# Layer boundaries with both norms from three sums per output tile, in a two-layer block followed by a second block

## The chip, the cores and the metric

One core of a Trainium2 chip runs the whole program in one launch. The metric is device time in microseconds of that core, from the start of the program to its end. The engines that matter here are TensorE (PE, matrix products), VectorE (DVE), ScalarE (ACT), GpSimd (POOL) and the DMA queues, above all SyncE's (SP), which streams the weights.

## What is computed

256 tokens of x and 256 tokens of ctx, 1024 features, two layers of a three-branch block (attention, a long convolution, a gated MLP), and then one layer of a second block on x alone. Everything is float32. What matters here lies where a layer ends and the next begins:

```python
for l in range(DEPTH):
    h  = rms_norm(x,  norm_pre[l]) * (1.0 + sc[:, None]) + sh[:, None]
    hc = rms_norm(xc, norm_pre[l]) * (1.0 + scc) + shc
    z  = h @ w_in[l]
    ...
    out   = merge_branches(z, (y_a, y_b, y_c), w_branch[l], w_out[l])   # ends with "out @ wo"
    x_new = x + gt[:, None] * rms_norm(out, norm_post[l])
    if not last:
        xc = xc + gtc * rms_norm(outc, norm_post[l])
    x = x_new
...
proj = rms_norm_2(x, g_mix[i]) @ w_in[i]      # second block, on x
```

So at each boundary there are two norms over the 1024 features of every token: one of the branch's output, and one of the new x, which is the old x plus the gated, normalized output.

## The kernel before

**Layout.** Activations lie with features on the 128 partitions: x is `self.x[:, k, :]`, k = 0 to 7 (KT = 8) blocks of 128 features, with 512 columns (ALL): 256 tokens of x (TOK), then 256 of ctx. Layer 0 works on 512 columns, layer 1's output and block 2 on 256. Weights come as tiles of 128 x 1024 in one fixed stream. `plan()` writes their order; a Tile has a number t, a kind ("wout", "q", "k", "v", "zc", "head", "cmp" ...) and a number of use, whose remainder by 4 is its PSUM bank among gemm_bank0 to 3. misc_bank0 to 3 (`self.M`) serve for the rest.

**Products in three parts.** Each float32 product is done as three in a rounded format (`three`, L417 to L419): both operands are split into hi and lo. For a weight tile SyncE loads `raw` (4 buffers, a load waits until the split four tiles before is done), ScalarE writes `whi` (`act_hi`, L1190; it waits until the tile four before is used up), VectorE writes `wlo` (`dve_lo`, L1711). ScalarE is three tiles ahead of TensorE, VectorE two.

**Programs.** Each engine has its own instruction list, written out by hand as one Python walk (`pe_...`, `act_...`, `dve_...`, `pool...`). `mark` increments a semaphore with an instruction, `at` gives the value that another engine waits for. An engine works in the order of its list, so a wait holds up all that follows on that engine. `pe_tiles(n)`, `act_tiles(n)` and `dve_tiles(n)` do the next n tiles' work on each engine; with `split=False` without the weight split ahead. A bank is free for a new tile when the copy out of it is done (`pe_bank`: it waits for "evac" of the use four before).

**End of a layer.** `pe_block1` runs eight wout tiles. ScalarE squares each (`act_sq`) and writes the gated output to `branch_out` (in the `halves` buffer); GpSimd adds the squares of tiles 0 to 6 (`pool_sums`, L2534), and TensorE sums over partitions with the constant `mean_all` (`pe_pooled`, L626 and L628). Beside the wout tiles of layer 0 there are tiles of kind "ada" (four products each pair, in four partition groups of one bank, L506) and the parts of layer 1's convolution filter: hidden layers, four taps (`pe_taps`, L663), squares, tap norm (`pe_tap_norm`, L677), spectrum (`pe_spec`, L694, and `dve_kern`).

**Boundary 0 to 1** (`pe_cross`, `act_cross`, `dve_cross`), first the x half (s = 0), then the ctx half (s = 1). VectorE takes reciprocals of the 256-column roots (L2224), scales the output and adds it to x for eight feature blocks (`dve_cross_new`, L2231 and L2232), ScalarE squares the new x (L1496), TensorE sums (L744), root, reciprocal, and then for each k VectorE forms the scaled input (L2239), ScalarE adds the shift and rounds (`act_cross_h`, L1505), VectorE writes the lo half (L2245). The four query tiles take the x half alone and go in the order QUAD, which starts tile after tile as the blocks k arrive; the four key tiles take both halves, in the order CROSS_KEYS of (tile, half). In `act_cross` each of four rounds squares some blocks and then does `act_tiles(1)`: one weight copy and one query bank copied out. After the keys come the four value tiles with tokens on the partitions, each of which writes all four banks, the angles and ropes on VectorE (`dve_trig`, `dve_rope`, L1975 to L1978), and the scores (L812), which wait for the last rope.

**Boundary 1 to block 2.** The same steps for 256 columns (L2314 and L2315, `act_sq`, `pe_sum` at L620, `dve_hn` at L2214 and L2218). `pe_block2` begins with waits for three constants (head_spread, ck_w2, cv_w2) that GpSimd loads (L2560 to L2562) behind its wait for the last "x_new", since their place held other data until then; then tiles zc 0, zc 1, head 0, 1, 2, with a sum for each head (`pe_head`, L974), and the compress tiles, for which ScalarE and VectorE first make up their other operand (`act_pair`, `dve_compress`).

Of the kernel before, what the change touches and what calls it, by code (L numbers as in the profile page):

```python
# [14 lines left out]
P = 128  # L15
# [18 lines left out]
CROSS_SUMS = (18, 20, 22, 24, 25, 27, 29, 31)  # L34
CROSS_SQ = ((0, 1, 2, 3, 4), (5,), (6, 7), ())
CROSS_KEYS = ((0, 0), (1, 0), (2, 0), (0, 1), (1, 1), (3, 0), (2, 1), (3, 1))
# [58 lines left out]
def plan():  # L95
# [33 lines left out]
    for l in range(DEPTH):  # L129
# [40 lines left out]
        if l == 0:  # L170
            extra["spec", 1] = uses
            uses += 1
# [45 lines left out]
POOLED = (("out", 0), ("out", 1), "g_ffn")  # L218


class Kernel:
# [82 lines left out]
    def memory(self):  # L304
# [24 lines left out]
        self.modA = sb("modA", [P, KT, 2])  # L329
        self.subg = [sb(f"sub_gain{l}", [P, 1]) for l in range(DEPTH)]  # L330
# [81 lines left out]
    def branch_out(self, k, s):  # L412
        return self.halves_f[:, k, s * ALL:s * ALL + TOK]

# [70 lines left out]
    def pe_tile(self, T):  # L485
# [25 lines left out]
        elif kind in ("k", "q", "hy", "gu", "gate", "esel", "zc", "head", "wout", "wout2", "pgate"):  # L511
            begun = {"k": ("h", T.l), "wout": ("merged", T.l), "zc": ("hn", "g_mix"), "wout2": ("merged", 2), "pgate": ("hn", "g_ple")}.get(kind)
# [130 lines left out]

    def hid(self, l):
        return self.tmp[0:64, 3, 0:TOK] if l else self.y[0:64, 0, 0:TOK]
# [9 lines left out]
    def pe_taps(self, l):  # L655
# [3 lines left out]
        for part in range(2):  # L659
            for t in range(2):  # L660
                if l == 0 and part and t:
                    pe.wait_ge(*self.at("root", "x0", 1))
                pe.matmul(self.tap_bank(l, 2 * part + t)[:, :], hid[:, t::2], self.hy_w3[:, part * BR:(part + 1) * BR], start=True, stop=True).then_inc(*self.mark("pe_filter", "taps_mm", l, 2 * part + t))  # L663

    def tap_bank(self, l, i):
        return self.M[i if l else (i + 1) % 4]
# [13 lines left out]
    def spec_bank(self, l, i):  # L680
        if l == 0:
            return self.M[i]
        return self.M[1 + i] if i < 3 else self.G[self.extra["spec", 1] % 4]

    def pe_spec(self, l):
        pe, sd = self.pe, self.tap_rows(l)[2]
        pe.wait_ge(*self.at("tap_root", l))
        pe.wait_ge(*self.at("tap_sd", l))
        pe.wait_ge(*self.landed("dft"))
        for part in range(2):  # L690
            for par in range(2):
                if l and part and par:
                    self.pe_bank(self.extra["spec", 1])
# [47 lines left out]
    def pe_cross_sum(self, s, k):  # L741

        self.pe.wait_ge(*self.at("sq", ("res", 0, s), k))
        self.pe.matmul(self.M[0][:, self.half(s)], self.c["mean_all"], self.tmp[:, k % 2, self.half(s)], start=(k == 0), stop=(k == KT - 1)).then_inc(*self.mark("pe_sum", "summed", ("res", 0, s), k))  # L744

    def pe_cross_queries(self, tiles):

        n = 0
        for step, (i, k) in enumerate(QUAD):
# [10 lines left out]
            if step in CROSS_SUMS:  # L760
                self.pe_cross_sum(1, CROSS_SUMS.index(step))

# [17 lines left out]
    def pe_cross(self):  # L780

        queries, keys = self.tiles[self.pe_next:self.pe_next + 4], self.tiles[self.pe_next + 4:self.pe_next + 8]
        for k in range(KT):
            self.pe_cross_sum(0, k)
        self.pe_cross_queries(queries)
        for i, side in CROSS_KEYS:
            self.pe_cross_keys(keys[i], side, (i, side) == (0, 1))
        self.pe_next += 8

    def pe_first(self):  # L790
# [3 lines left out]
        self.pe_tiles(2)  # L794
        self.pe_tap_norm(0)
# [134 lines left out]
    def pe_block1(self, l):  # L930
# [15 lines left out]
        for o in range(KT):  # L946
# [11 lines left out]
        if l == 0:  # L958
            self.pe.wait_ge(*self.at("taps", 1))
        self.pe_sum(("out", l), KT - 1, n)  # L960
        if l == 0:
            self.pe_tap_norm(1)
            self.pe_spec(1)
            self.pe_cross()
            return
        self.pe.wait_ge(*self.at("rstd", ("out", l)))
        for k in range(KT):
            self.pe_sum(("res", l), k, n)
# [103 lines left out]
    def pe_block2(self):  # L1072
# [5 lines left out]
        pe.wait_ge(*self.at("rstd", ("res", 1)))  # L1078
        self.pe_tiles(2)
        self.pe_heads(3)  # L1080
# [1720 lines left out]
```

## Time and profile before

| | |
|---|---|
| median of 3 timed runs | 1439.62 us (1439.2 to 1440.12) |
| profiled execution, its own time | 1443.96 us |
| its span | 1442.6 us, 20879 instructions |
| TensorE busy | 1381.1 us (96%), weight loads beside it 1166.8 us |
| VectorE, ScalarE, GpSimd busy | 936.2 (65%), 688.9 (48%), 41.8 us (3%) |
| granted TensorE clock, mean | 0.981 of 2.4 GHz |

Times in the profile are microseconds from the span's start. A line such as L1711 is that of the instruction in the kernel; where a helper issues all of one kind, one line stands for many. In a timeline each row gives the start, the duration, the engine, the line and operation, output <- inputs by the program's names, shapes and a count of merged instructions, and in brackets how long the engine was idle before it and what ended that. Matrix products overlap: one of 512 columns in the rounded format lasts 0.39 us, and the next starts 0.23 us after it; with 256 columns 0.28 and 0.12. A float32 product stands as two instructions. Layer 0 ends at 627 us and layer 1 at 970 us.

### The profile page before, as it was taken

How to read it: one execution, taken by the hardware profiler on the slowest of the kernel's cores; microseconds unless marked ns; L12 is line 12 of the kernel's file. 1: busy time of each engine (PE TensorE's matmuls, PEld its weight loads, DVE VectorE, ACT ScalarE, POOL GpSimd, SP SyncE). 2: the span in 40 equal slices, each digit the busy share in tenths (PEclk: the TensorE clock that was granted, in tenths of full speed). 3: DMA queues.
4: the chain of work that ended last, by engine and by line, in shares of the span. 5: the costliest groups of instructions: out<-in, count | busy, mean ns of one | idle time of the engine just before them, and what ended most of it. 6: DMA issues, size and time to landing. Idle time of an engine off the chain costs nothing.

```text
span 1442.6 us, 20879 instructions
## 1 busy us (share of the span) xinstructions
PE 1381.1 (96%) x8318; PEld 1166.8 (81%) x8318; DVE 936.2 (65%) x1687; ACT 688.9 (48%) x1190; POOL 41.8 (3%) x50
## 2 busy tenths in 40 slices
PE   5999999999999999989999999998999999999998
PEld 2577668778888888669789899997889999888888
DVE  4574664876423344388875777658867777888556
ACT  5433545234322232454356454465656746666444
POOL 0000000000000000100000000010000002000001
PEclk8999999999999999999999999998999999999999
DMA  9332343144332232622233355553633245655552
GB/s 364 137 102 73 144 148 103 44 171 158 102 102 88 90 100 81 215 77 89 78 126 133 124 191 194 186 176 109 212 136 116 92 145 176 199 186 193 197 175 74
DMA packets 57793, 202.21 MB, mean 140 GB/s; under 512 B 6272, under 2 KB 9536, under 8 KB 57696
## 3 DMA queue, kind: packets, MB, share of 16 engines
q1 hardware_dynamic: 55568, 194.01, 39.9%
q0 software_dynamic: 1760, 6.12, 1.3%
q8 instruction: 66, 1.08, 0.3%
q10 hardware_dynamic: 368, 0.74, 0.2%
q14 instruction: 31, 0.25, 0.1%
HBM read 199.80 MB, written 1.05 MB: 139 GB/s over the span
## 4 chain that ended last, share of the span: by engine, by line
PE 83%; DVE 10%; ACT 3%; DMA 2%; issue 1%; ACTq 0%; SPq 0%; DVEq 0%
PE gemm_bank L417 16%; PE gemm_bank L419 15%; PE gemm_bank L418 15%; PE misc_bank L417 4%; PE misc_bank L418 4%; PE misc_bank L419 4%; PE misc_bank L428 3%; PE gemm_bank L428 3%; DVE wlo L1711 2%; PE gemm_bank L573 1%; PE misc_bank L573 1%; PE misc_bank L429 1%; PE gemm_bank L429 1%; PE gemm_bank L506 1%; PE misc_bank L853 1%; PE misc_bank L812 1%
## 5 line engine op out<-in xcount | busy, mean ns | idle before, releaser
L1711 DVE TENSOR_TENSOR wlo<-raw,whi 128x1024 fp32r<-128x1024 f32 x316 | 382.9, 1223 | 76.6 <-ACT whi L1190 73.2
L1190 ACT ACTIVATE whi<-raw 128x1024 fp32r<-128x1024 f32 x316 | 332.8, 1055 | 163.1 <-PE gemm_bank L419 95.8
L417 PE MATMUL gemm_bank<-halves,wlo 128*128 128x256 f32 (+1 forms) x1152 | 376.5, 327 | 18.7 <-DVE halves L2175 5.2
L418 PE MATMUL gemm_bank<-halves,whi 128*128 128x256 f32 (+1 forms) x1152 | 361.4, 314 | 0.0
L419 PE MATMUL gemm_bank<-halves,whi 128*128 128x256 f32 (+1 forms) x1152 | 361.3, 314 | 0.0
L417 PEld LDWEIGHTS gemm_bank<-halves,wlo 128*128 128x128 f32 x1152 | 223.6, 194 | 42.6 <-issue 17.8
L419 PEld LDWEIGHTS gemm_bank<-halves,whi 128*128 128x128 f32 x1152 | 224.0, 194 | 12.0
L418 PEld LDWEIGHTS gemm_bank<-halves,whi 128*128 128x128 f32 x1152 | 224.4, 195 | 11.3 <-issue 0.7
L417 PE MATMUL gemm_bank<-arena_r,wlo 128*128 128x512 f32 (+1 forms) x320 | 108.3, 338 | 1.9 <-DVE wlo L1711 1.9
L419 PE MATMUL gemm_bank<-arena_r,whi 128*128 128x512 f32 (+1 forms) x320 | 107.6, 336 | 0.0
L418 PE MATMUL gemm_bank<-arena_r,whi 128*128 128x512 f32 (+1 forms) x320 | 107.5, 336 | 0.0
L417 PE MATMUL misc_bank<-halves,wlo 128*128 128x512 f32 (+1 forms) x288 | 101.9, 354 | 0.0
L418 PE MATMUL misc_bank<-halves,whi 128*128 128x512 f32 (+1 forms) x288 | 101.9, 354 | 0.0
L419 PE MATMUL misc_bank<-halves,whi 128*128 128x512 f32 (+1 forms) x288 | 101.9, 354 | 0.0
L1746 DVE SCALAR_TENSOR_TENSOR tmp<-tmp,gemm_bank 128x512 f32<-128x512 f32 (+1 forms) x28 | 16.1, 574 | 97.4 <-ACT tmp L1259 97.4
L1259 ACT ACTIVATE tmp<-misc_bank 128x512 f32<-128x512 f32 (+1 forms) x36 | 19.0, 527 | 121.3 <-PE misc_bank L419 121.3
L417 PEld LDWEIGHTS gemm_bank<-arena_r,wlo 128*128 128x128 f32 x320 | 60.7, 190 | 11.2 <-DVE wlo L1711 3.5
L419 PEld LDWEIGHTS gemm_bank<-arena_r,whi 128*128 128x128 f32 x320 | 60.7, 190 | 6.3
L418 PEld LDWEIGHTS gemm_bank<-arena_r,whi 128*128 128x128 f32 x320 | 60.8, 190 | 6.1
L428 PE MATMUL gemm_bank<-halves,whi 128*128 128x512 f32 x176 | 62.2, 395 | 0.0
L428 PE MATMUL misc_bank<-halves,whi 128*128 128x512 f32 x176 | 62.1, 394 | 0.0
L417 PEld LDWEIGHTS misc_bank<-halves,wlo 128*128 128x128 f32 x288 | 54.5, 189 | 7.5
(419 smaller groups left out, 2271.8 us busy)
## 6 DMA issues: line engine op xcount, KB each, us to landing
raw<-in_stream SPq DMA_DIRECT2D x348, 512.0 KB, 3.3
arena<-in_stream SPq DMA_DIRECT2D x16, 512.0 KB, 11.6
x<-in_x SPq DMA_DIRECT2D x1, 1024.0 KB, 6.8
x<-in_ctx SPq DMA_DIRECT2D x1, 1024.0 KB, 10.2
y<-in_hy_decay POOLq DMA_DIRECT2D x2, 512.0 KB, 4.1
arena<-in_gm_ws POOLq DMA_DIRECT2D x2, 512.0 KB, 5.8
const_b<-in_const_b POOLq DMA_DIRECT2D x1, 635.0 KB, 5.8
y<-in_hy_w POOLq DMA_DIRECT2D x2, 256.0 KB, 3.5
```

Source lines behind the costliest of these rows:

```text
L417: mm(out, w_lo, r_hi, start=first, stop=False)
L418: mm(out, w_hi, r_lo, start=False, stop=False)
L419: return mm(out, w_hi, r_hi, start=False, stop=last)
L428: self.pe.matmul(bank[:, :], hi[:, c], self.hi_lo(k, s), start=(k == 0), stop=False)
L429: m = self.pe.matmul(bank[:, 0:TOK], lo[:, c], self.hi(k, s), start=False, stop=(k == KT - 1))
L506: m = pe.matmul(bank[c:c + 32, :], self.cond_w[:, 2 * q + kk, :], raw[:, kk * BR:(kk + 1) * BR], start=(q < 2), stop=(q >= 2), tile_positi ...
L573: pe.matmul(self.out_banks[o][:, :], hi[:, c], self.ah_al[:, j, :], start=(j == 0), stop=False)
L812: mm = pe.matmul(self.M[m][:, 0:nkeys], self.Q[r, h, q], self.K[r, h, k_off:k_off + nkeys], start=True, stop=True)
L1190: act.activation(self.whi[:, t % SPLIT, :], self.raw_tile(t), ACT.Copy).then_inc(*self.mark("tile_hi", "tile_hi", t))
L1259: act.activation(self.tmp[:, e % 2, 0:n], self.M[e][:, 0:n], ACT.Tanh, scale=0.5).then_inc(*self.mark("act_sel", "sel_tanh", T.use))
L1711: dve.tensor_tensor(self.wlo[:, t % SPLIT, :], self.raw_tile(t), self.whi[:, t % SPLIT, :].bitcast(F32), ALU.subtract).then_inc(*self.mark ...
L1746: self.own(dve.scalar_tensor_tensor(th, th, 1.0, b[:, 0:n], ALU.add, ALU.mult))
```

## The change

Three products per wout tile instead of one square. For the gated output b (after the gate, `branch_out`), the raw output o and the old x, TensorE sums over features o*o, x*b and b*b. They go into the partition groups 0 to 31, 32 to 63 and 64 to 95 of misc_bank0 (`pe_norm_sum`). ScalarE squares o, VectorE forms x*b and b*b one tile later (`dve_branch`). With r = 1/sqrt(mean o*o + eps) the energy of the new x is E(x) + 2 r (x.b) + r^2 (b.b), so the second norm is known as soon as the first is. The three rows are copied to SBUF, transposed so that each token is a partition, and both factors are worked out as columns (`act_norm`, `dve_norm_factors`). Each is spread over all partitions again by a product with the identity (`pe_norm_spread`). E(x) of the input comes from its root once, at the start (`pe_input_energy`, `dve_input_energy`). GpSimd's sums at the two boundaries go, and so do the squares of the new x and their sums.

VectorE then goes block by block: scale b, form the next input, add to x, write the lo half (`dve_cross_rows`, `dve_last_rows`). At the last boundary the first four tiles run in the order QUAD (`pe_last_quad`). The taps are split over two wout tiles, the spectrum over the place before the queries and the place after the keys. The core of the diff:

```diff
-CROSS_KEYS = ((0, 0), (1, 0), (2, 0), (0, 1), (1, 1), (3, 0), (2, 1), (3, 1))
+CROSS_KEYS = ((0, 0), (1, 0), (2, 0), (3, 0), (0, 1), (1, 1), (2, 1), (3, 1))
-POOLED = (("out", 0), ("out", 1), "g_ffn")
+POOLED = ("g_ffn",)
...
+    def pe_norm_sum(self, l, j, n):
+        pe = self.pe
+        for q, src in enumerate(self.norm_rows(j, n)):
+            pe.wait_ge(*self.at(("sq", "xb", "bb")[q], ("out", l), j))
+            m = pe.matmul(self.by_half(self.M[0][32 * q:32 * q + 32, 0:n], n), self.c["mean_all"][:, 0:32], src, start=(j == 0), stop=(j == KT - 1), tile_position=(0, 32 * q))
+        m.then_inc(*self.mark("pe_sum", "summed", ("out", l), j))
+    def pe_norm_turn(self, l, n):
+        self.pe.wait_ge(*self.at("norm_rows", l))
+        for i in range(n // P):
+            m = self.pe.transpose(self.M[0][:, 96 * i:96 * i + 96], self.tmp[0:96, 2, i * P:(i + 1) * P], self.ident[0:96, 0:96])
+    def pe_norm_spread(self, l, s, i):
+        pe.wait_ge(*self.at("norm_r", l, i))
+        if s:
+            pe.wait_ge(*self.at("h", l + 1, 0, KT - 1))
+        for e in range(2):
+            r = self.norm_r[:, 4 * i + 2 * s + e:4 * i + 2 * s + e + 1]
+            m = pe.matmul(self.spread_bank(i)[:, e * P:(e + 1) * P], r.broadcast_to([P, P]), self.ident, start=True, stop=True)
...
     def pe_cross_queries(self, tiles):
-            if step in CROSS_SUMS:
-                self.pe_cross_sum(1, CROSS_SUMS.index(step))
+            if step == 2 * KT + 7:
+                for r in range(2):
+                    self.pe_norm_spread(0, 1, r)
     def pe_cross(self):
-        for k in range(KT):
-            self.pe_cross_sum(0, k)
+        self.pe_norm_turn(0, ALL)
+        self.pe_spec(1, 0, 1)
+        for r in range(2):
+            self.pe_norm_spread(0, 0, r)
         self.pe_cross_queries(queries)
         for i, side in CROSS_KEYS:
             self.pe_cross_keys(keys[i], side, (i, side) == (0, 1))
+        self.pe_spec(1, 1, 2)
...
     def pe_block1(self, l):
             if o:
-                self.pe_sum(("out", l), o - 1, n)
+                self.pe_norm_sum(l, o - 1, n)
             if l == 0 and o == 4:
-                self.pe_taps(1)
+                self.pe_taps(1, range(3))
+            if l == 0 and o == 5:
+                self.pe_taps(1, range(3, 4))
...
     def pe_block2(self):
         pe.wait_ge(*self.landed("head_spread"))
         pe.wait_ge(*self.landed("ck_w2"))
         pe.wait_ge(*self.landed("cv_w2"))
-        pe.wait_ge(*self.at("rstd", ("res", 1)))
-        self.pe_tiles(2)
-        self.pe_heads(3)
+        self.pe_last_quad()
+        self.pe_tiles(1)
+        for n in range(2):
+            self.pe_head(n)
...
+    def act_norm(self, l, n):
+        act.wait_ge(*self.at("summed", ("out", l), KT - 1))
+        act.activation(self.tmp[0:96, 2, 0:n], self.M[0][0:96, 0:n], ACT.Copy).then_inc(*self.mark("act_root", "norm_rows", l))
+        act.wait_ge(*self.at("norm_cols", l))
+        act.activation(self.norm_r[:, 0:n // P], self.norm_cols(0, n), ACT.Sqrt, bias=self.c["eps"]).then_inc(*self.mark("act_root", "root_out", l))
+        act.wait_ge(*self.at("energy", l))
+        act.activation(self.norm_r[:, 4:4 + n // P], self.energy[:, 0:n // P], ACT.Sqrt, bias=self.c["zero"]).then_inc(*self.mark("act_root", "root_new", l))
     def act_cross(self):
+        self.act_norm(0, ALL)
         act.wait_ge(*self.at("mod", 1))
-        self.act_cross_h(0)
+        self.act_cross_h(0, 0, 1)
+        self.act_kern(1, 0)
+        self.act_cross_h(0, 1, KT)
         for i in range(4):
-            for k in CROSS_SQ[i]:
-                self.act_cross_sq(1, k)
-            self.act_tiles(1)
-        act.wait_ge(*self.at("summed", ("res", 0, 1), KT - 1))
-        self.act_cross_root(("res", 0), 1)
-        self.act_cross_h(1)
+            self.act_hi()
+            self.act_cross_h(1, i, i + 1)
+        self.act_tiles(4, split=False)
+        self.act_cross_h(1, 4, KT)
     def act_block1(self, l):
         if l:
             self.act_tiles(1, split=False)
+            self.act_kern(1, 1)
             self.act_tiles(4)
...
+    def dve_branch(self, l, j, n):
+        v, out = self.dve, self.both_halves(j, 0, n)
+        _, xb, bb = self.norm_rows(j, n)
+        for s in range(n // TOK):
+            v.wait_ge(*self.at("branch", l, j, s))
+        if j >= 2:
+            v.wait_ge(*self.at("summed", ("out", l), j - 2))
+        v.tensor_tensor(xb, out, self.by_half(self.x[:, j, 0:n], n), ALU.mult).then_inc(*self.mark("dve_norm", "xb", ("out", l), j))
+        v.tensor_tensor(bb, out, out, ALU.mult).then_inc(*self.mark("dve_norm", "bb", ("out", l), j))
+    def dve_cross_rows(self, s):
+        v = self.dve
+        v.wait_ge(*self.at("spread_r", 0, s, 0))
+        for k in range(KT + 2):
+            if k < KT:
+                self.dve_scaled(0, s, k)
+            if k == 1:
+                v.wait_ge(*self.at("spread_r", 0, s, 1))
+            if 1 <= k <= KT:
+                self.dve_cross_sum(s, k - 1)
+            if k < KT:
+                self.dve_new(0, s, k)
+            if k >= 2:
+                self.dve_cross_lo(s, k - 2)
+            if s == 0 and k == 4 or s and k < 4:
+                self.dve_lo()
+            if s == 0 and k == 8:
+                self.dve_tap_rs(1)
     def dve_block1(self, l):
         if l:
             self.dve_tiles(6, split=False)
-            self.dve_tiles(2)
+            self.dve_tiles(1)
+            self.dve_kern(1, 1, 2)
+            self.dve_tiles(1)
...
     def gpsimd_program(self):
-            self.pool_sums(("out", l), TOK if l else ALL)
-        pool.wait_ge(*self.at("x_new", DEPTH - 1, KT - 1))
+        pool.wait_ge(*self.at("x_new", DEPTH - 1, 0, KT - 1))
         pool.dma_start(self.head_spread, ins["head_spread"]).then_inc(*self.landing("head_spread"))
```

`dve_last_rows` has the same loop as `dve_cross_rows` for the 256 columns of the last boundary, with one `dve_lo` at k = 5. `pe_last_quad` is the loop of `pe_cross_queries` over the tiles zc 0, zc 1, head 0 and head 1. `act_block2` begins with the rounding of the eight blocks, one weight copy and the copies of the two zc banks. `dve_norm_factors` is a chain of operations on columns: reciprocal, product, product with addition, product, then one addition per group of 128 tokens, and behind ScalarE's second root another reciprocal.

## Rows read from the trace of the kernel before

**Rows 1.** The page: chain by engine; the two costliest groups of other engines.

```profile
PE 83%; DVE 10%; ACT 3%; DMA 2%; issue 1%; ACTq 0%; SPq 0%; DVEq 0%
...
L1711 DVE TENSOR_TENSOR wlo<-raw,whi 128x1024 fp32r<-128x1024 f32 x316 | 382.9, 1223 | 76.6 <-ACT whi L1190 73.2
L1190 ACT ACTIVATE whi<-raw 128x1024 fp32r<-128x1024 f32 x316 | 332.8, 1055 | 163.1 <-PE gemm_bank L419 95.8
```

**Rows 2.** Busy time by stretch; behind POOL the granted clock, DMA share, GB/s.

```profile
643.30:650.00 6.70, 6.66 (x32) 6.67 (x33) 6.52 (x15) 3.06 (x6) 0.00 (x0) 0.53 0.26 81
650.00:657.00 7.00, 7.00 (x54) 6.78 (x53) 5.84 (x16) 2.66 (x6) 0.00 (x0) 1.00 0.00 1
```

**Rows 3.** Timeline, TensorE: start us, duration us, engine line op xcount [idle before <-releaser].

```profile
598.61 0.39 PE L419 MATMUL gemm_bank<-arena_r,whi 128*128 128x512 f32 x1
598.92 1.06 PE L506 MATMUL gemm_bank<-raw,cond_w 128*32 128x512 f32 x8
599.92 0.50 PE L417 MATMUL gemm_bank<-arena_r,wlo 128*128 128x512 f32 x1
...
627.17 1.02 PE L626 MATMUL misc_bank<-sq_sum,const_a 128*128 128x512 f32 x2
...
628.98 0.95 PE L677 MATMUL misc_bank<-const_a,arena 128*128 128x1 f32 x8
630.28 2.84 PE L694 MATMUL misc_bank<-y,shared 128*128 128x512 f32 x6 [0.35 <-ACT hy_rs L1341]
...
643.34 0.55 PE L417 MATMUL gemm_bank<-halves,wlo 128*128 128x256 f32 x1 [4.15 <-DVE halves L2245]
```

**Rows 4.** Timeline, VectorE, around the end of layer 0.

```profile
616.54 0.68 DVE L1872 TENSOR_TENSOR arena<-misc_bank,y 128x512 f32<-128x512 f32 x1
...
631.99 0.43 DVE L2232 TENSOR_TENSOR x<-x,halves_f 128x256 f32<-128x256 f32 x1
632.34 0.42 DVE L2231 TENSOR_TENSOR halves_f<-halves_f,tmp 128x256 f32<-128x256 f32 x1
...
643.12 0.48 DVE L2239 SCALAR_TENSOR_TENSOR tmp<-x,modA,tmp 128x256 f32<-128x256 f32 x1
643.51 0.48 DVE L2245 SCALAR_TENSOR_TENSOR halves<-tmp,mod,halves 128x256 fp32r<-128x256 f32 x1
```

**Rows 5.** Timeline, ScalarE, last wout tile of layer 0.

```profile
627.86 1.02 ACT L1270 ACTIVATE halves_f<-gemm_bank,const_a,mod 128x256 f32<-128x256 f32 x2
```

**Rows 6.** Timeline, VectorE and TensorE, from the keys' end to the scores.

```profile
680.22 1.80 DVE L1850 SCALAR_TENSOR_TENSOR tmp<-tmp 128x256 f32<-128x256 f32 x4
683.21 1.23 DVE L1711 TENSOR_TENSOR wlo<-raw,whi 128x1024 fp32r<-128x1024 f32 x1 [1.18 <-ACT whi L1190]
...
684.24 0.40 PE L417 MATMUL gemm_bank<-whi,halves 128*128 128x512 f32 x1
...
709.63 0.70 PE L812 MATMUL misc_bank<-arena 64*128 64x512 f32 x2 [3.44 <-DVE arena L1978]
```

**Rows 7.** Timeline, layer 1 to block 2; one row of the DMA issues.

```profile
970.14 0.59 PE L626 MATMUL misc_bank<-sq_sum,const_a 128*128 128x256 f32 x2
...
979.83 0.42 DVE L2315 TENSOR_TENSOR x<-x,halves_f 128x256 f32<-128x256 f32 x1
...
981.63 0.54 POOL L2562 DMA_DIRECT2D shared<-in_cv_w  x1
...
shared<-in_cv_w POOLq DMA_DIRECT2D x1, 64.0 KB, 3.1
...
985.98 0.55 PE L417 MATMUL gemm_bank<-halves,wlo 128*128 128x256 f32 x1 [3.87 <-DVE halves L2218]
...
994.44 0.39 ACT L1222 ACTIVATE arena<-gemm_bank 128x256 f32<-128x256 f32 x1 [1.53 <-PE gemm_bank L419]
...
1001.10 0.38 ACT L1277 ACTIVATE tmp<-gemm_bank 128x256 f32<-128x256 f32 x1
...
1003.54 0.47 PE L417 MATMUL gemm_bank<-whi,cmp_xl 128*30 128x256 f32 x1
```

More of the change, by code:

```diff
@@ L658, in pe_taps @@
         pe.wait_ge(*self.landed(f"hy_w3{l}"))
[L659 to L663, printed above, removed]
+        for i in some:
+            part, t = divmod(i, 2)
+            if l == 0 and i == 3:
+                pe.wait_ge(*self.at("root", "x0", 1))
+            if l and i == 3:
+                pe.wait_ge(*self.at("tap_out", l, 0))
+            pe.matmul(self.tap_bank(l, i)[:, :], hid[:, t::2], self.hy_w3[:, part * BR:(part + 1) * BR], start=True, stop=True).then_inc(*self.mark("pe_filter", "taps_mm", l, i))
     def tap_bank(self, l, i):
-        return self.M[i if l else (i + 1) % 4]
+        return self.M[1 + i % 3 if l else (i + 1) % 4]
     def tap_rows(self, l):
@@ L794, in pe_first @@
         self.pe_tiles(2)
+        self.pe_input_energy()
         self.pe_tap_norm(0)
@@ L1565, in act_block1 @@
             return
-        self.act_root(("out", l), n)
-        for k in range(KT):
-            act.wait_ge(*self.at("x_new", l, k))
-            self.act_sq(("res", l), k, n, self.x[:, k, 0:n]).then_inc(*self.mark("act_sq", "sq", ("res", l), k))
+        self.act_hi()
+        self.act_norm(1, TOK)
     def act_pair(self, which, z):
@@ L1784, in dve_tile @@
                 self.dve_half("g_ffn", j - 1, 1)
+        elif kind == "wout":
+            if j:
+                self.dve_branch(l, j - 1, n)
         elif kind == "ffg":
@@ L1874, in dve_taps @@
                 self.own(m)
-                v.memset(a[0:1, 2, :], 0.0)
-        m.then_inc(*self.mark("dve_filter", "taps", l))
+                m = v.memset(a[0:1, 2, :], 0.0)
+            if l and i == 0:
+                m.then_inc(*self.mark("dve_filter", "tap_out", l, i))
+        if 3 in some:
+            m.then_inc(*self.mark("dve_filter", "taps", l))
     def dve_tap_add(self, l):
@@ L2225, in dve_cross_rstd, with dve_scaled @@
         self.dve.wait_ge(*self.at("rstd", stage, s))
[L2227 to L2240 removed]
+    def dve_scaled(self, l, s, k):
+        out = self.branch_out(k, s)
+        self.dve.tensor_tensor(out, out, self.spread_bank(0)[:, 0:TOK], ALU.mult).then_inc(*self.mark("dve_x", "out_scaled", l, s, k))
@@ new lines, in dve_new, with dve_cross_sum @@
+    def dve_new(self, l, s, k):
+        x = self.x[:, k, self.half(s)]
+        self.dve.wait_ge(*self.at("out_scaled", l, s, k))
+        self.dve.tensor_tensor(x, x, self.branch_out(k, s), ALU.add).then_inc(*self.mark("dve_x", "x_new", l, s, k))
+    def dve_cross_sum(self, s, k):
+        self.dve.wait_ge(*self.at("x_new", 0, s, k))
+        self.dve.scalar_tensor_tensor(self.tmp[:, (0, 1, 3, 4)[k % 4], self.half(s)], self.x[:, k, self.half(s)], self.modA[:, k, s:s + 1], self.spread_bank(1)[:, 0:TOK], ALU.mult, ALU.mult).then_inc(*self.mark("dve_h", "h_sum", 1, s, k))
@@ L2251, in dve_cross @@
[L2251 to L2264 removed]
+        self.dve_norm_factors(0, ALL)
@@ new lines, in dve_last_rows @@
+    def dve_last_rows(self):
+        v = self.dve
+        self.dve_branch(1, KT - 1, TOK)
+        self.dve_lo()
+        self.dve_norm_factors(1, TOK)
+        v.wait_ge(*self.at("spread_r", 1, 0, 0))
+        for k in range(KT + 2):
+            if k < KT:
+                self.dve_scaled(1, 0, k)
+            if k == 1:
+                v.wait_ge(*self.at("spread_r", 1, 0, 1))
+            if 1 <= k <= KT:
+                self.dve_last_sum(k - 1)
+            if k < KT:
+                self.dve_new(1, 0, k)
+            if k >= 2:
+                self.dve_last_lo(k - 2)
+            if k == 5:
+                self.dve_lo()
+        self.dve_lo()
@@ L2310, in dve_block1 @@
             return
-        self.dve_rstd(("out", l), n)
-        for k in range(KT):
-            out = self.branch_out(k, 0)
-            self.own(v.tensor_tensor(out, out, self.tmp[:, 2, 0:n], ALU.mult))
-            v.tensor_tensor(self.x[:, k, 0:n], self.x[:, k, 0:n], out, ALU.add).then_inc(*self.mark("dve_x", "x_new", l, k))
     def dve_compress(self, which):
```

204 lines of the change are left out of this document (109 added, 95 removed).

## The prediction

> **What bounds the kernel now.** I read the page first. TensorE (PE) holds 83% of the chain that ended last and VectorE (DVE) 10% [rows 1], so a microsecond added to TensorE's program counts in full, and one taken from another engine counts only where TensorE waits for it. The waits of TensorE then show where that is. At the end of layer 0 the last wout tile is through at 627.17, which I call A, and the first product of layer 1 starts at 643.34, A+16.2 [rows 3]. In between come the pooled sum, a reciprocal of 256 columns, eight pairs of "scale, add", eight squares with their sums, and two more reciprocals. After it the granted clock is 0.53 for some six microseconds, that is mostly the lower level of 1.2 GHz, then 1.00 [rows 2]; the engine had waited 4.15 us just before. A stretch of six microseconds at the lower level costs about 2.7 us of the work that it holds. At the end of layer 1 the last wout tile is through at 970.14, which I call B, and the first product of block 2 starts at 985.98, B+15.8 [rows 7]. A third wait hangs on the first: VectorE works from 683.21 without a gap (splits, angles, ropes) up to the last rope, for which the scores wait 3.44 us; they start at 709.63, 25.4 us after the keys ended at 684.24 [rows 6].
>
> **Sums inside wout.** Before, GpSimd added the squares. After, TensorE makes three 512-column products behind each output tile. The nearest row is the pair of ada tiles: four products into four partition groups, eight instructions. The tile before is through at 598.84 (its last product's start and the 0.23 us from one to the next), the next tile's first product starts at 599.92 [rows 3]. The first of the eight lasts as long as one, so the groups run side by side. I take 1.1 us for three; side by side without any cost of changing over it would be 0.85 (the 512-column sum begun at 627.17), one behind the other 2.55. Seven lie ahead of A: +7.7 us. Tile 6's sum also waits. VectorE after tile 5 must do the last tap product, two tap sums, a split (1.22, [rows 1]) and two products of 0.68 [rows 4], 8.6 us in all, against 7.9 us of TensorE work: +0.7. Layer 1 has 256 columns: 7 x 0.6 = +4.2. The sum of the input's energy adds four products like L677's, 0.95 [rows 3]: +1.0, beside nothing. Together +13.6 us (9 to 29).
>
> TensorE's page in the Trainium skill ("TensorE: Matmul & The Clock Gate", Measured speedup vs the span model) gives 2.38 times for three column groups, and its tiling page ("TensorEngine Tiling (Array Packing)", Key Properties) says that a change of mode drains the engine. By the first an estimate is 2.55/2.38 = 1.07 us a group; the second would come on top, but the ada row holds such a change already.
>
> **From A to the first rows of layer 1.** ScalarE (ACT) writes both halves in 1.02 us [rows 5], VectorE multiplies twice (A+2.6), the last sum ends at A+3.6, then copy, four transposes, root, reciprocal (A+5.4). TensorE meanwhile runs two spectrum products (three took 2.55 us, [rows 3]) and spreads the first factor at A+7.0, the second at A+7.6. Nothing of 256 columns is left of roots and reciprocals. VectorE now works in rows: scale 0.35, layer input 0.40, add 0.34, split 0.40 [rows 4], 1.49 us a row, and the first row is whole three rows in: A+10.8 instead of 16.2. That is the gain. But the old program made these rows at 0.79 us each once begun, so the eighth row comes at A+21.0 (with one weight split between), before it was A+22.5. The queries end at A+26.9 (11.5 us of work, starved at first and then partly at the lower clock).
>
> **The keys must wait for the queries' banks.** This is the step that decides. In act_cross the four query banks are now copied out by act_tiles(4) behind four rounds of "act_hi, act_cross_h(1, i)", where before one was copied in each round. The keys take those same banks. Their rows for the second half start when TensorE has spread that half's factors, behind step 23 of the queries: about A+24.0 (22.5 to 25). VectorE scales and adds row 0 and splits key 0's weights: +2.05. Each further round is scale 0.35, layer input 0.48, ScalarE's rounding 0.5, its weight copy 1.05 and VectorE's split 1.22 [rows 1], with the handovers 3.65 us; three of them, then the fourth layer input, rounding and one copy (1.75): the first bank is free at +14.75, A+38.8. TensorE has nothing from A+26.9, 12 us. Then come eight half tiles and again the lower clock (2.7). Half a tile takes 2.88 us: from 643.34 to 684.24 the old program did twelve of them, eight sums of 0.43 (half the columns of the 0.85) and the clock's 2.7 [rows 3, 6]. So the keys end at A+64.5. Before, they ended at A+57.1. **+7.4 us** (3 if no clock is lost and the spread comes early, 9 at the other end).
>
> **Values and ropes.** The second half of the spectrum now follows all keys (1.7 us), and ScalarE's kern copy stands in act_block1 ahead of the first weight copy of the values. So their weights, ready before the keys' end in the old program, are copied from the keys' end+2.5 on and split by +4.8; TensorE waits 3 us. Behind that, VectorE has kern 1.3, a split 1.2, the angles 3.5 (four steps of 1.80 together and five of a third) and then the same gapless 26.4 us up to the scores [rows 6]: 3.6 + 1.2 + 1.3 + 1.2 + 3.5 + 26.4 = keys' end+37.2, where it was +25.4. The value tiles are done by +27, so the scores' wait grows from 3.4 to some 10 us. **+11.8 us** (10 to 13), the 1.7 and the 3 included. What hid them before was that VectorE began them 1.0 us ahead of the keys' end; now it is 10.8 us behind it.
>
> **Block 2.** Here the four first tiles go through pe_last_quad as rows come (first row B+8.6, eighth B+18.7). But pe_block2 still begins with the waits for head_spread, ck_w2 and cv_w2, which GpSimd loads only behind the last x_new. Before, that was 980.25, the last DMA was issued at 981.63 and landed 3.1 us later, 984.7, ahead of the rows; it cost nothing [rows 7]. Now the last x_new stands in round 7 of the row loop: B+16.9, with a landing at B+21.4. TensorE starts at B+21.6, not at B+15.8, with all rows there, and needs 14.2 us for four tiles (11.5 and 2.7 of clock): B+35.8, before B+29.9. ScalarE, too, can copy the first bank only after that tile's end, and from the second bank's copy (994.44) to the end of head 1's square (1001.48) it needed 7.0 us [rows 7]; from B+33.9 with two mask copies of 0.5 that is B+41.4, and TensorE's two head sums wait for it. The compress tiles start at B+41.8, before at 1003.54, B+33.4: **+8.4 us** (5.5 to 10). A later wait of 2 us for loads may shrink: -1.
>
> **Sum.** 13.6 + 7.4 + 11.8 + 8.4 - 1 = 40.2 us. The profiled execution had a span of 1442.6 us and a time of 1443.96; the three timed runs have a median of 1439.62, 0.3% less, which I take as the same shift for both kernels: 1439.6 + 40.2 = 1480.
>
> **Rivals.** (1) Each late wait above is off the path, and the change does what its design wants. Then the keys end at A+53 (the weight splits and the last row at A+44 decide), the second spectrum costs 1.7 on TensorE, the ropes' wait of 3.4 us goes, and block 2 has its four tiles by B+23.5, 6.4 earlier: 13.6 - 4.1 + 1.7 - 3.4 - 6.4 = +1.4, 1441 us, no change; with sums at 0.85 us instead of 1.1 and no fall of the clock at either start (2.7 each) it is faster, 1433. For it speaks the row at A+10.8; against it, that bank, copy and load each stand in one engine's program order. It decides from the point where the first query bank is copied before A+30. Chance 0.07, half of it with a gain that can be measured. (2) One of the three big waits does not come or is given back later (the bank, the ropes, or the loads): 1458 to 1472. Chance 0.15. (3) The three sums run one after the other: 7 x 1.45 in layer 0 and 7 x 0.7 in layer 1, +15 us, 1495. Against it speaks the ada row. Chance 0.06. My forecast, 1472 to 1490, has 0.72.
>
> Range 1456 to 1491; it leaves out most of rival 1 and of rival 3 and holds a little over 8 in 10. A measurement of this kernel can tell about 0.2% (2.9 us) from no change. Faster 0.04, same 0.04, slower 0.92.
>
> **What would show it.** In the profile after: a group of three 32-column products at about 1.1 us behind each wout tile; the first product of layer 1 some 11 us after the last wout tile; a gap of 10 to 13 us ahead of the first key product, ended by ScalarE's copy of a query bank; some 3 us ahead of the first value product, ended by a weight split; some 10 us before the scores, ended by a rope; and a first product of block 2 that starts when cv_w2 has landed, 4.5 us after the last x_new. If the key gap is under 3 us, or the first product of block 2 comes near B+9, I am wrong by the amounts given.

## The result and the profile after

The changed kernel takes 1476.32 us (median of 4 runs, 1474.22 to 1481.52), the kernel before 1439.41 beside it: a ratio of 1.0259 with a 95% interval of 1.0233 to 1.0284, so 2.6% slower. Run again later, the changed kernel gave 1477.5 us and 1.0246 (1.0224 to 1.0268). The profiled execution has a span of 1473.5 us, its own time is 1474.9.

The waits of TensorE in the changed kernel, between 560 and 740 us and between 960 and 1060 us (what waited, for what, us in total, times, longest):

```profile
PE gemm_bank L433 <- ACT arena L1291: 10.8, 1, 10.8
PE misc_bank L862 <- DVE arena L2084: 7.2, 1, 7.2
...
PE gemm_bank L433 <- DVE wlo L1773: 2.9, 1, 2.9
...
PE gemm_bank L433 <- DMA shared<-in_ck_w: 14.7, 1, 14.7
```

The first is the wait for the copy out of a query bank, the second that for the last rope (3.44 before [rows 6]), the third the value weights' split, the last the constants that GpSimd loads. All four are where the prediction put them, at the sizes it gave but for the rope's (some 10 us predicted, 7.2 measured). The instructions at their ends, and the start of layer 1 (timeline, TensorE):

```profile
629.82 0.62 PE L665 MATMUL misc_bank<-tmp,const_a 128*32 128x512 f32 x1
...
636.24 1.44 PE L683 MATMUL misc_bank<-const_a,norm_r 128*128 128x128 f32 x8
640.49 0.36 PE L433 MATMUL gemm_bank<-halves,wlo 128*128 128x256 f32 x1 [2.81 <-DVE halves L2340]
...
651.55 1.05 PE L683 MATMUL misc_bank<-const_a,norm_r 128*128 128x128 f32 x8
...
666.29 0.55 PE L433 MATMUL gemm_bank<-halves,wlo 128*128 128x256 f32 x1 [10.82 <-ACT arena L1291]
...
692.00 1.88 PE L744 MATMUL misc_bank<-y,shared 128*128 128x512 f32 x4
696.77 0.80 PE L433 MATMUL gemm_bank<-whi,halves 128*128 128x512 f32 x1 [2.89 <-DVE wlo L1773]
728.90 2.08 PE L862 MATMUL misc_bank<-arena 64*128 64x512 f32 x4 [7.20 <-DVE arena L2084]
...
1014.41 0.55 PE L433 MATMUL gemm_bank<-halves,wlo 128*128 128x256 f32 x1 [14.74 <-DMA shared<-in_ck_w]
...
1034.79 0.78 PE L433 MATMUL gemm_bank<-whi,cmp_xl 128*30 128x256 f32 x1
```

Layer 1 does start early: the last wout tile is through at 629.73 (A) and the first product comes at 640.49, A+10.8, where it was A+16.2 [rows 3]. All of that gain and more is then lost. The same stages in both profiles of each kernel (the unchanged kernels were profiled a second time), worked out from TensorE's timeline; "keys" is the end of the last key product, "cmp" the first compress product:

| us | before | before again | after | after again | difference |
|---|---|---|---|---|---|
| first ada pair beside wout to A | 50.8 | 50.5 | 55.7 | 55.7 | +5.1 |
| A to first product of layer 1 | 16.2 | 16.2 | 10.8 | 10.8 | -5.4 |
| A to keys | 57.1 | 56.1 | 62.3 | 61.2 | +5.2 |
| keys to scores | 25.4 | 25.4 | 36.9 | 36.9 | +11.5 |
| scores to B | 260.5 | 260.0 | 265.0 | 264.6 | +4.5 |
| B to cmp | 33.4 | 32.9 | 40.9 | 40.4 | +7.5 |
| cmp to the end | 439.1 | 442.0 | 438.7 | 440.5 | -0.9 |

The stages (the second row is part of the third) add up to +32.9. What lies ahead of the first mark makes -0.8 more (the mark comes at 576.4 and 576.0 before, at 574.0 and 576.8 after), and the profiled spans differ by 30.9 and 33.4. The medians differ by 36.9 and 36.1. The rest lies in which execution was profiled: those of before took 1443.96 and 1444.03 us, 2.6 to 4.5 above the median beside them, the first of after 1.4 less than its median.

### The profile page after: what moved, and what is told of

Its sections match the earlier page's. It is cut to its first block, busy times and chain, and to the rows that moved or that the text cites. A ratio compares the mean times of both kernels' runs of the same rounds, so it can differ in the third digit from the quotient of the medians.

```text
span 1473.5 us, 21034 instructions
## 1 busy us (share of the span) xinstructions
PE 1385.8 (94%) x8396; PEld 1164.3 (79%) x8396; DVE 939.8 (64%) x1732; ACT 677.9 (46%) x1166; POOL 27.3 (2%) x38
## 4 chain that ended last, share of the span: by engine, by line
PE 83%; DVE 11%; ACT 3%; issue 1%; DMA 1%; ACTq 0%; POOL 0%; DVEq 0%
PE gemm_bank L433 16%; PE gemm_bank L435 15%; PE gemm_bank L434 15%; PE misc_bank L433 4%; PE misc_bank L435 4%; PE misc_bank L434 4%; PE misc_bank L444 3%; PE gemm_bank L444 3%; DVE wlo L1773 2%; PE misc_bank L445 1%; PE gemm_bank L445 1%; PE gemm_bank L589 1%; PE misc_bank L589 1%; PE misc_bank L862 1%; PE misc_bank L903 1%
## 5 line engine op out<-in xcount | busy, mean ns | idle before, releaser
L433 PE MATMUL gemm_bank<-halves,wlo 128*128 128x256 f32 (+1 forms) x1152 | 375.4, 326 | 40.0 <-DMA shared<-in_ck_w 14.7
L444 PE MATMUL gemm_bank<-halves,whi 128*128 128x512 f32 x176 | 63.4, 400 | 0.0
L434 PEld LDWEIGHTS misc_bank<-halves,whi 128*128 128x128 f32 x288 | 54.5, 189 | 7.5
```

What stands on the lines that cost most here:

```text
L433: mm(out, w_lo, r_hi, start=first, stop=False)
L434: mm(out, w_hi, r_lo, start=False, stop=False)
L444: self.pe.matmul(bank[:, :], hi[:, c], self.hi_lo(k, s), start=(k == 0), stop=False)
```

## Experiments

Each is the changed kernel with one edit, or a sum of such edits; the last three sums build on one another.

**The bank.** ScalarE copies each query bank in its round:

```diff
         for i in range(4):
             self.act_hi()
             self.act_cross_h(1, i, i + 1)
-        self.act_tiles(4, split=False)
+            self.act_tiles(1, split=False)
```

> One edit to the changed kernel: ScalarE copies each query bank out in its own round behind act_cross_h(1, i), not all four behind the rounds. My theory (the keys wait only for the copy of the first query bank): the first key product comes right behind the queries, the 10.8 us wait of TensorE goes, and the keys then end when the ctx rows (last one at 671.9) and three and a half half tiles of 2.88 us allow it, 681 to 684 in place of 692; all later waits stay as they are. About 1467 us, 9 less than 1476 (7 to 11). Rival (the rows of the ctx half or the weight splits would hold the keys as long anyway): the wait only changes its name, 1473 to 1476.

Measured: 1467.33 us (ratio to before 1.0182, 1.0156 to 1.0208), 9.0 less. The first key product starts at A+26.2 in place of A+36.6 and the keys end at A+52.1, 10.1 earlier and 4.9 ahead of the kernel before; keys to scores is 36.9 still. Timeline of TensorE in this kernel, the first product of the queries behind the second spread of factors, then the first product of each of the first four key halves:

```profile
652.86 0.36 PE L433 MATMUL gemm_bank<-halves,wlo 128*128 128x256 f32 x1
656.39 0.36 PE L433 MATMUL gemm_bank<-halves,wlo 128*128 128x256 f32 x1 [0.42 <-ACT arena L1291]
660.13 0.36 PE L433 MATMUL gemm_bank<-halves,wlo 128*128 128x256 f32 x1 [0.63 <-ACT arena L1291]
663.87 0.36 PE L433 MATMUL gemm_bank<-halves,wlo 128*128 128x256 f32 x1 [0.63 <-ACT arena L1291]
667.61 0.36 PE L433 MATMUL gemm_bank<-halves,wlo 128*128 128x256 f32 x1 [0.65 <-ACT arena L1291]
```

Each key half starts about 3.7 us behind the last, the length of a round, and waits 0.4 to 0.65 us for its own bank. The wait of 10.8 us is gone and has not only changed its name, as the rival had it: the bank was the cause.

**The spectrum.** Its second half goes between queries and keys, its copy on ScalarE behind the query banks, its part on VectorE behind the ctx rows:

```diff
         self.pe_cross_queries(queries)
+        self.pe_spec(1, 1, 2)
         for i, side in CROSS_KEYS:
             self.pe_cross_keys(keys[i], side, (i, side) == (0, 1))
-        self.pe_spec(1, 1, 2)
...
+        self.act_kern(1, 1)
         self.act_cross_h(1, 4, KT)
...
             self.dve_cross_rows(s)
-        self.dve_kern(1, 0, 1)
+            self.dve_kern(1, s, s + 1)
```

(act_kern(1, 1) and dve_kern(1, 1, 2) go from their old places in act_block1 and dve_block1.)

> One edit to the changed kernel: the second half of the spectrum is computed between queries and keys, where TensorE is idle, its ScalarE copy behind the query banks' copies, its VectorE part behind the ctx rows; nothing of it is left behind the keys. My theory (the two products, the copy and the delayed weight splits are all that puts values and ropes behind): the 2.9 us wait and the 1.9 us of products ahead of the first value product go, and the scores come some 25 us after the end of the keys as before and not 36.9. About 1465 us, 11.5 less (9 to 13). Rival (the ropes are behind because the copies of the key banks come late, not because of the spectrum): only the 1.9 and 2.9 us ahead of the values go and come back as a longer wait for the ropes, 1476.

Measured: 1468.47 us (1.0200, 1.0170 to 1.0231), 7.9 less, under the 9 to 13 expected and far from the rival's no change. The value products follow the keys without a wait, and keys to scores falls from 36.9 to 27.1, by 9.8 of the 11.5. The scores still wait, for a rope:

```profile
719.39 2.08 PE L862 MATMUL misc_bank<-arena 64*128 64x512 f32 x4 [5.18 <-DVE arena L2084]
```

**The loads.** The three waits of pe_block2 go from its head to just ahead of the kc_mm products:

> One edit to the changed kernel: TensorE waits for head_spread, ck_w2 and cv_w2 only ahead of the first product that reads one of them, no longer ahead of the first four tiles of block 2. My theory: the first product of block 2 starts about 8.6 us after the last wout tile in place of 20.6, the four tiles end 3 to 5 us behind the last row (about 22.5 us after it) in place of 37.5, and the compress tiles come 12 us earlier. About 1464 us (1462 to 1468). Rival (the chain of bank copies, head squares and the compress operand on ScalarE and VectorE holds the compress tiles whatever TensorE does): 7.5 us at most come back, 1469 or more.

Measured: 1470.21 us (1.0201, 1.0175 to 1.0227), 6.1 less. By the time alone this is what the rival said (1469 or more), but the stage did what was expected and refutes it. Timeline of TensorE: the first product at B+8.4, and the compress tiles at B+28.2 in place of B+40.9, 12.7 earlier:

```profile
1006.80 0.55 PE L433 MATMUL gemm_bank<-halves,wlo 128*128 128x256 f32 x1 [2.61 <-DVE halves L2380]
```

But cmp to the end is 444.9 here and 438.7 in the changed kernel. The stretches show where (busy time of the engines, then PEclk as the third number from the end); first this kernel, then the changed one at the same work:

```profile
1102.00:1112.00 10.00, 9.45 (x52) 8.08 (x52) 7.48 (x29) 3.92 (x10) 0.00 (x0) 0.66 0.43 147
...
1218.00:1224.00 6.00, 5.48 (x33) 5.49 (x34) 3.49 (x6) 2.73 (x6) 0.00 (x0) 0.72 0.52 172
```

```profile
1109.00:1119.00 10.00, 9.45 (x77) 8.61 (x77) 7.88 (x34) 6.79 (x21) 0.00 (x0) 1.00 0.50 160
...
1226.00:1232.00 6.00, 6.00 (x53) 6.00 (x52) 3.91 (x6) 3.97 (x7) 2.86 (x2) 1.00 0.68 237
```

Two stretches partly at 1.2 GHz, in which TensorE falls back 2.9 and 1.5 us against the changed kernel; 1.2 us more is a slower pace of the second set of paired products (last section: one lasts 399 ns here, 392 in the changed kernel), and 0.6 I did not trace. The first of them stands in both profiles of before, in this kernel and in the next; in none of the six profiles that have the long wait ahead of block 2; and not in the last three kernels below either, which start block 2 as early as this one. So the early start alone doesn't bring it, and what sets it stays open. The second comes and goes within one kernel: the granted clock is 0.67 at 1224 to 1228 in the second profile of the changed kernel and 0.58 at 1192 to 1196 in the second of before, and neither has such a stretch in its first profile. The 6.1 us between two medians of four runs, each of which spreads over 6 to 7 us, are themselves uncertain by some 2 to 3 us.

**All three.**

> The three edits of the other kernels of this call together. If the three waits are apart from each other, their gains add: 9 + 11.5 + 12 = 32.5 us, 1444 us (1440 to 1450), and what is left against the kernel before is the price of the sums less what the earlier first rows give: within 10 us of 1439.4. If one feeds the next (a start that comes earlier only meets the same late row or rope), the gains overlap: 1455 or more.

Measured: 1452.26 us (1.0075, 1.0049 to 1.0100), 24.1 less. A to keys is 53.5, keys to scores 27.1, B to cmp 28.2: 31.3 us less in the three stages than in the changed kernel, of which scores to B (+1.2) and the tail (+5.9, with the same two stretches at the lower clock) take back 7. So the three waits are nearly apart from each other (their gains one by one are 10.1, 9.8 and 12.7, together 8.8, 9.8 and 12.7), and the result lies between the two expectations because of what came behind them.

**What the sums cost.** Both kernels change only pe_norm_sum, and neither computes the norms that the reference asks for. The first leaves out the partition groups: each of the three products goes to all 96 columns, in turn, so that the three sums are added into one:

```diff
-            m = pe.matmul(self.by_half(self.M[0][32 * q:32 * q + 32, 0:n], n), self.c["mean_all"][:, 0:32], src, start=(j == 0), stop=(j == KT - 1), tile_position=(0, 32 * q))
+            m = pe.matmul(self.by_half(self.M[0][0:96, 0:n], n), self.c["mean_all"][:, 0:96], src, start=(j == 0 and q == 0), stop=(j == KT - 1 and q == 2))
```

> One edit to the changed kernel: the three products of each norm sum write the same 96 columns of output one after the other, not three groups of 32 side by side; the sums are then no longer the three that the norms need, which is left as it is. My theory (three groups side by side cost about 0.97 us with 512 columns and 0.57 with 256): in turn they cost 3 x 0.85 and 3 x 0.43, 1.6 and 0.7 more each, six and seven times on the path: +14.5 us, 1490 to 1492. Rival (my third one of the prediction, the groups run in turn anyway): no change, 1476.

Measured: 1494.4 us (1.0355, 1.0335 to 1.0375), 18.1 more. The wout stage of layer 0 grows by 9.1 us, which is 1.5 for each of six groups; A to keys by 2.4, as two groups lie behind A, which the expectation left out; scores to B by 2.8. That is 14.3 us in one profile, the quickest of the four executions, as expected; the medians are 3.8 us further apart. The changed kernel's groups do run side by side. The second leaves out most of the sums: the first and the last group of a layer become one product with 96 output columns, and the six between one product of a single column:

> One edit to the changed kernel: of the eight norm sums of each layer only the first and the last are made, with one product of 96 output columns each, the six between are one product of a single column; all waits stay. The norms are then not those of the reference. What the sums cost is read off directly. By the trace of the changed kernel six groups ahead of the end of layer 0 cost 0.97 us each and 0.6 of stall, those of layer 1 0.57 each, and two groups lie behind each layer's last tile: about 8 us less, 1468 us (1466 to 1470). Rival (the sums fill time that TensorE would lose to waits anyway, as the 1.9 us wait for a weight split in layer 0 before): 3 us less at most.

Measured: 1470.29 us (1.0200, 1.0178 to 1.0223), 6.0 less: 3.8 in the wout stage of layer 0 and 3.1 between scores and B. The waits for VectorE's products come out in their place: 0.6 us ahead of A, and 1.6 and 1.5 us ahead of the last sums, which lie behind A and B, so that nothing is gained there (the first product of layer 1 comes at A+10.9). Taking the sums out gives back 6 to 7 us; the expectation of 8 was high, its rival of 3 low.

**Key order.** e4_all with CROSS_KEYS as before:

> The three edits of e4_all, and the order of the key half tiles as in the kernel before, (3, 0) behind (1, 1) and not ahead of (0, 1). My theory (the last 1.8 us between the end of the keys and the scores, 27.2 against 25.4, come from the later release of key 1's weight buffers): the wait for the last rope is 3.4 us again, 1450.5 us. Rival (the order only moves the wait ahead of the ctx rows, since the first ctx row comes late): no change or 1 us more.

Measured: 1449.14 us (1.0058, 1.0034 to 1.0082). Keys to scores is 25.4 and the rope's wait 3.4, as expected; in turn TensorE waits 2.7 us more for ctx rows within the keys. Stage by stage nothing is gained (A to scores 81.7, in e4_all 80.6). Its eight runs fall into two groups by the granted clock: four at 0.991 or 0.992 took 1444.2 to 1447.1 us, four at 0.979 to 0.984 took 1451.2 to 1458.4. The profiled one is of the first group, all runs of e4_all are at 0.982 to 0.986, and so the 3 us between the medians aren't evidence. Nor is the missing stretch at the lower clock in this profile.

**Cheaper sums.** The kernel of the key order, with the products of pe_norm_sum in the rounded format, with a constant `mean_r` whose middle 32 of 160 columns are 1/1024 and the rest zero:

```diff
+            m = pe.matmul(self.by_half(self.M[0][0:96, 0:n], n), self.mean_r[:, 64 - 32 * q:160 - 32 * q], src, start=(j == 0 and q == 0), stop=(j == KT - 1 and q == 2))
```

> e7_order and cheaper sums: squares and products are written in the rounded format, and three one-pass products in turn, each with a 96-column weight that is the constant in its own 32 columns and zero in the others, write all three sums. Three times 0.23 and 0.12 us in place of 0.97 and 0.57, and no change of the array's mode: 0.3 us less for each of six, 0.2 for each of seven, and the stall of 0.6: 3 to 4 us less than e7_order, 1447 us. If the change of mode costs nothing and the stalls stay, 1 us less. It would beat the kernel before only if the waits left (3.6 us ahead of the first rows, 3.4 for the ropes) were smaller too; I don't expect it.

Measured: 1443.45 us (1.0015, 1.0004 to 1.0027). By the profiles the wout stage is 0.5 us shorter and the first product of layer 1 comes at A+10.2 instead of A+10.8; a wait of 0.98 us for a weight split, which the longer sums had covered, is back. The median is 5.7 us lower than e7_order's, but the two profiles differ by little over 1 us from the first mark to the end, the 1 us of the expectation's alternative and not the 3 to 4 of its theory. They don't compare at one clock, either: the twelve runs here are at 0.979 to 0.984, like e7_order's slower four, and are some 10 us below those (median 1453.2) and 2 below its quicker four (1445.5). What of this is the sums' isn't shown.

**Idle places of VectorE.** The kernel of the cheaper sums with three moves; the first of them:

```diff
             self.dve_tiles(6, split=False)
-            self.dve_tiles(1)
-            self.dve_tiles(1)
             self.dve_trig(0, 0)
-            self.dve_tiles(1)
+            self.dve_tiles(2)
             self.dve_trig(0, 1)
+            self.dve_tiles(1)
```

> e8_fast and three small moves: VectorE works out the first angle while it would wait for the value weights (it stood idle for 1.4, 2.8 and 1.2 us there), which brings the last rope 3.4 us forward, so that the 3.4 us wait ahead of the scores goes; the sum of block 2's head 1 goes behind the first compress tile (0.98 us of wait); and at both boundaries the lo half of a row is written ahead of the next addition (0.35 us each). 4.5 us less than e8_fast, 1439 us, 2 us under the kernel before. If the value products end where the ropes ended, or the clock takes back part of it, 1 to 2 us less than e8_fast, no difference to the kernel before.

Measured: 1439.81 us (12 runs) against 1441.45 of before (17 runs), ratio 0.9983, 0.9970 to 0.9995: 0.2% faster than the kernel before, with an interval that just leaves out no change. The wait ahead of the scores is gone (keys to scores 22.0), the first product of layer 1 is at A+9.9, the compress tiles at B+27.2.

**The unchanged kernels again.**

> The changed kernel once more, unaltered, for a second profile. My theory on the tail of block 2 (in e3_loads it lost 6.2 us against the changed kernel behind the compress tiles, 3.0 of it a stretch at the lower clock that kernels with a long wait ahead of block 2 do not show and 1.5 of it a second one; the pace of the paired products changes from run to run): the second profile has no low stretch between 1070 and 1130 either, while the pace of the paired products may differ. Rival (all of it is chance from run to run): the low stretches lie elsewhere. Median 1476 us as before.

> The kernel before once more, unaltered, for a second profile. The same question: a low stretch some 20 us behind the last head sum of block 2 as in the first profile if it belongs to the kernel, none if it is chance; paired products at 0.346 us a pair as in the first profile, or at 0.354 as in the others. 1440 us.

Measured: 1477.50 us and, in one run, 1444.03. In the second profiles the changed kernel again has no stretch at the lower clock between 1070 and 1130, the kernel before again has one, at 1076 to 1084. By these four alone it would belong to the kernels; the seven profiles with an early start, which are split, speak against that. The pace of the paired products of block 2, which might have differed from run to run, is the same in both profiles of each kernel (last section).

## Why the prediction was right

The time (1480, measured 1476.3) and the sign were right. The sum was 40.2 us; the medians say 36.9, the stages 32.9.

**Sums (13.6; stages 5.1 + 4.5 = 9.6).** The groups were sized well: a group of three with 512 columns, from its start to the next tile's first product (timeline, TensorE):

```profile
597.46 0.59 PE L665 MATMUL misc_bank<-tmp,const_a 128*32 128x512 f32 x1
...
597.89 0.59 PE L665 MATMUL misc_bank<-tmp,const_a 128*32 128x512 f32 x1
598.42 0.51 PE L433 MATMUL gemm_bank<-arena_r,wlo 128*128 128x512 f32 x1
```

0.96 us, taken as 1.1. (Three in turn are 2.55, a ratio of 2.66; the Trainium skill, "TensorE: Matmul & The Clock Gate", Measured speedup vs the span model, has 2.38, and an estimate by it is 1.07. The measurement decides.) The count was wrong: the sum of tile 6 is issued behind tile 7, so six groups lie ahead of A, not seven. And one wait was not looked up: before, TensorE waited 1.85 us in this stage for a weight split, and the added work covers it:

```profile
586.56 0.50 PE L417 MATMUL gemm_bank<-arena_r,wlo 128*128 128x512 f32 x1 [1.85 <-DVE wlo L1711]
```

The stall came too, 0.6 us (the group behind tile 6 starts at 622.57 and the next tile at 624.14). 6 x 0.96 + 0.6 - 1.85 is 4.5, measured 5.1. In layer 1, too, six groups lie ahead of B and not seven. There two groups are 3.63 us apart (972.18 and 975.80 in TensorE's timeline), of which the tile's 24 products make 2.88 at 0.12 us each: a group with its handovers costs 0.75, not 0.6, and 6 x 0.75 is the measured 4.5. The two errors cancel (4.2 predicted). The products for the input's energy run at 79.1 to 79.8, ahead of the first mark; that mark comes anywhere from 573.8 to 578.1 in the thirteen profiles, so the 1.0 us for them can't be told.

**First rows (A+10.8; measured A+10.8).** Right.

**Keys (+7.4; measured +5.2).** The mechanism is confirmed by e1_banks. The first key product was put at A+38.8 and came at A+36.6. The second factors were spread at A+21.8, not A+24.0, since step 23 of the queries was reached sooner; from there to the first key product it is 14.7 us, as worked out (38.8 - 24.0). The eight half tiles took 25.7 us, as predicted, the lower clock at their start included; it stands at 0.50 from 660 on, before they start at 666.3 (stretches of the changed kernel, PEclk the third number from the end):

```profile
660.00:672.00 12.00, 5.71 (x27) 5.74 (x28) 11.03 (x26) 4.98 (x11) 0.00 (x0) 0.50 0.29 101
672.00:680.00 8.00, 8.00 (x68) 8.00 (x68) 1.08 (x2) 0.00 (x0) 0.00 (x0) 0.99 0.00 0
```

**Values and ropes (+11.8; measured +11.5).** TensorE waits 2.9 us for the value weights (3 predicted), and the scores come 36.9 us behind the keys (37.2 predicted). The value tiles are done at the keys' end+29.7 and not +27, with the granted clock at 0.57 from 696 to 704; the ropes end last, so it costs nothing. e2_spec takes 9.8 us away. The other 1.7 go with the new key order (e7_order: 25.4), and fit with a later release of key 1's weight buffer: the value weights' split behind the first angle starts 1.0 us ahead of the keys' end in e7_order and 0.7 us behind it in e4_all. But e7_order's keys end later, and its scores come no earlier after A. The prediction had no term for the order, and put it all down to the spectrum.

**Block 2 (+8.4; measured +7.5).** Start at B+20.6 (21.6 predicted), compress tiles at B+40.9 (41.8). e3_loads confirms the cause: without it B+28.2, where rival 1 had put them at 33.4 - 6.4 = B+27.

**Behind the compress tiles (-1; measured -0.9).** The size is luck. The term was to be a shorter wait for loads, but no wait of TensorE for a load stands there in either kernel. What stands there is a slower pace of the paired products (+2.3, last section) against the stretch at the lower clock, which the profiles of before have and those of after don't; in the first pair of profiles it is worth 2.8 us.

**Rivals.** Rival 1, that every late wait is off the path, is refuted by the rows; the design without the three waits is e4_all, which is 11 us above rival 1's 1441. Its keys end at A+53.5 (53 predicted) and its compress tiles come at B+28.2 (27), but keys to scores is 27.1, not 25.4 - 3.4 + 1.7 = 23.7, the sums cost what they cost, and the tail lost 5.9. Rival 3 is what e5_serial built: 1494.4, where it had said 1495; the changed kernel is 18.1 us below it. Rival 2 did not occur.

**Profile and medians.** The same shift of 0.3% for both kernels was assumed. It wasn't so: before lay 0.3% above its median when profiled, after at or below it. That, and not a further mechanism, is why a sum that is 7 us above the stages came out 3 us above the medians. Part of this agreement is luck.

## What to carry to other kernels

Before a boundary is rearranged, follow each PSUM bank, each weight buffer and each late load to the instruction that frees it, and ask who stands behind it: a copy moved from inside a loop to behind it cost 9 to 10 us here, a wait left at the head of a block 12.7 us of its stage, two small products, a copy and two VectorE steps moved behind a stage 9.8. When work is added to the engine that sets the time, look up the waits that it will cover, and count what lies on each side of the mark from which you measure.

## What was not expected of the hardware

In the paired products of block 2 (512 columns, then 256), which no edit touches and which wait for nothing there at a granted clock of 1.00, the pace differs from kernel to kernel. Groups by line and shape, from 1100 to 1440 us before and from 1130 to 1470 after:

```profile
L428 PE MATMUL gemm_bank<-halves,whi 128*128 128x512 f32 x176 | 62.2, 395 | 0.0
```

```profile
L444 PE MATMUL gemm_bank<-halves,whi 128*128 128x512 f32 x176 | 63.4, 400 | 0.0
```

With its twin in misc_bank this is 2.3 us over the stage (from the first to the last product of the twin 119.8 us before, 122.1 after). Both profiles of before, e8_fast and e9_more have the quick pace (62.2), both of after and e1 to e7 the slow one (63.4): in these thirteen profiles it goes with the program, and it is 2.3 of the 36.9 us. The next stage's pairs are quick or slow within one kernel (394 ns in one profile of before, 399 in the other). The cause wasn't looked into; no wait and no clock that the profile shows goes with it. A few us between two kernels can lie in work that the change doesn't touch.
